# Order of VectorE's low parts and a landing wait on SyncE in the expert stage of a hybrid encoder layer

## The reference

```
expert group = top 1 of 4, then top 2 of its 8 experts, per token
rows sorted by expert, each expert's rows padded to blocks of 128
for each block:  hid = silu(xb @ w_eg[e]) * (xb @ w_eu[e]);   ys = hid @ w_ed[e]
out[token] += ys * gate
```

## Time and profile before

| | |
|---|---|
| time, median of 3 runs | 1236.81 us (1235.13 to 1236.97) |
| the profiled execution | 1234.7 us, span 1232.8 us |
| busy | PE 90%, PEld 78%, DVE 59%, ACT 46%, POOL 26% |
| chain that ended last | PE 78%, DVE 10%, ACT 5% |
| expert stage | from about 804 us to 1189 us of the span |

### The profile page before, as it was taken

One profiled execution on the slowest core, in us unless ns is written; L12 is line 12 of the kernel. 1 busy time (PEld: TensorE's weight loads), 2 busy tenths in 40 slices (PEclk: granted clock), 3 DMA queues, 4 the chain that ended last, 5 costly groups with the idle time before them and its releaser, 6 DMA issues.

```text
span 1232.8 us, 18548 instructions
## 1 busy us (share of the span) xinstructions
PE 1110.1 (90%) x6851; PEld 961.3 (78%) x6851; DVE 730.7 (59%) x948; ACT 563.7 (46%) x759; POOL 325.0 (26%) x273
## 2 busy tenths in 40 slices
PE   3998999999999899999998999758999999999930
PEld 3886888888877788888887788657999999999930
DVE  5874666666044621111113465568888888888838
ACT  5334655665135200000003232336888888888823
POOL 3203222212332223223330000032444444444210
PEclk7998999999999999999999999968999999999975
DMA  8010000020204111111103342348999999999747
GB/s 247 1 28 11 7 7 7 6 70 18 69 1 106 37 29 44 52 52 52 52 12 108 108 171 86 154 175 316 377 373 349 347 347 361 360 379 365 263 153 282
DMA packets 94174, 184.31 MB, mean 150 GB/s; under 512 B 30752, under 2 KB 68128, under 8 KB 80288
## 3 DMA queue, kind: packets, MB, share of 16 engines
q1 hardware_dynamic: 83744, 166.65, 38.9%
q0 software_dynamic: 10368, 16.80, 3.7%
HBM read 177.12 MB, written 27.26 MB: 166 GB/s over the span
## 4 chain that ended last, share of the span: by engine, by line
PE 78%; DVE 10%; ACT 5%; issue 3%; DMA 3%; SPq 1%; POOL 0%; ACTq 0%; DVEq 0%; POOLq 0%
PE ps L376 24%; PE ps L378 23%; PE ps L377 23%; PE ps L900 3%; PE ps L668 2%; DVE pt_lo L1382 1%; PE ps L829 1%; DVE negm L1337 1%; DVE q_tmp L1328 1%; ACT prob L1032 1%; DMA xin<-in_x_dram 1%; DVE acc L1688 1%; DVE res L1698 1%; DVE acc L1689 1%; PE ps L677 1%
## 5 line engine op out<-in xcount | busy, mean ns | idle before, releaser
L1639 DVE TENSOR_TENSOR we_lo<-raw_e,we_hi 128x2048 fp32r<-128x2048 f32 x108 | 246.8, 2287 | 51.2 <-ACT we_hi L1159 51.1
L1159 ACT ACTIVATE we_hi<-raw_e 128x2048 fp32r<-128x2048 f32 x108 | 205.8, 1908 | 0.0
L376 PE MATMUL ps<-ht_hi,w_hi 128*128 128x512 f32 x448 | 176.0, 393 | 0.5 <-DVE ht_lo L1255 0.4
L378 PE MATMUL ps<-ht_hi,w_lo 128*128 128x512 f32 x448 | 174.5, 390 | 0.0
L377 PE MATMUL ps<-ht_lo,w_hi 128*128 128x512 f32 x448 | 174.4, 389 | 0.0
L376 PE MATMUL ps<-we_hi,xst_hi 128*128 128x256 f32 x576 | 169.8, 295 | 1.9 <-DVE xst_lo L1643 1.9
L377 PE MATMUL ps<-we_lo,xst_hi 128*128 128x256 f32 x576 | 163.8, 284 | 0.0
L378 PE MATMUL ps<-we_hi,xst_lo 128*128 128x256 f32 x576 | 163.8, 284 | 0.0
L370 POOL CAST w_hi<-raw 128x1024 fp32r<-128x1024 f32 x36 | 40.5, 1125 | 301.6 <-PE ps L378 268.8
L376 PEld LDWEIGHTS ps<-we_hi,xst_hi 128*128 128x128 f32 x576 | 111.6, 194 | 2.5 <-DVE xst_lo L1643 2.4
L377 PEld LDWEIGHTS ps<-we_lo,xst_hi 128*128 128x128 f32 x576 | 111.4, 193 | 0.0
(11 more groups left out here) (293 smaller groups left out, 2495.8 us busy)
## 6 DMA issues: line engine op xcount, KB each, us to landing
raw_e<-in_w_exp_gate_dram SPq DMA_DIRECT2D x36, 1024.0 KB
raw_e<-in_w_exp_up_dram SPq DMA_DIRECT2D x36, 1024.0 KB
raw_e<-in_w_exp_down_dram SPq DMA_DIRECT2D x36, 1024.0 KB
raw<-in_w_in_dram SPq DMA_DIRECT2D x27, 512.0 KB, 3.8
yin<-y_dram SPq DMA_DIRECT2D x16, 512.0 KB, 6.7
xin<-in_x_dram SPq DMA_DIRECT2D x8, 512.0 KB, 7.0
raw<-in_w_out_dram SPq DMA_DIRECT2D x8, 512.0 KB, 3.9
xre<-in_x_dram SPq DMA_DIRECT2D x8, 512.0 KB, 5.7
```

Source lines behind the costliest of these rows:

```text
L376: pe.matmul(dst, st[0], mv[0], start=first, stop=False)
L378: return pe.matmul(dst, st[1], mv[0], start=False, stop=last)
L1159: act.activation(we_hi[c % 4][:, :], raw_e[c % 6][:, :], ACT.Copy).then_inc(sem("w_hi_ready"), 1)
L1639: dve.tensor_tensor(we_lo[c % 4][:, :], raw_e[c % 6][:, :], we_hi[c % 4][:, :].bitcast(F32), ALU.subtract).then_inc(sem("w_lo_ready"), 1)
```

## The change

On VectorE the low part of the gathered rows (`rows_low`) is no longer the last step of a block for block j + 3: it is now called with j + 2 right behind `hidden_low(it, j)`, ahead of the split of the up piece. Since one block's last step and the next one's first steps follow each other, this is a swap of `rows_low` and `hidden_low`. In the prologue `hidden_low(0, 0)` moves ahead of the split `low(0, 0, 2)`, of `rows_low(0, 2)` and of the gate operations.

On SP, `load` now also waits until piece p - 2 has landed in full before it issues piece p (from the seventh piece on).

```
@@ load, on SP
-                    wait(sp, "w_lo_ready", n - 5)
+                    if isinstance(it, int):
+                        split, arrived = n - 5, (it * 2 + ((c - 2) // 6 + 1)) * 16
+                    else:
+                        split, arrived = sp.to_reg(n - 5), sp.to_reg((it * 2 + ((c - 2) // 6 + 1)) * 16)
+                    if not (isinstance(it, int) and n < 6):
+                        sp.wait_ge(sem(f"raw_e_full{(c - 2) % 6}"), arrived)
+                    wait(sp, "w_lo_ready", split)
@@ expert, on VectorE
-                    hidden_low(it, j)
+                    if not (isinstance(it, int) and it == 0 and j == 0):
+                        hidden_low(it, j)
                     if left(2):
+                        rows_low(it, j + 2)
                         low(1, it, j + 2)
                     if left(1):
                         hidden(it, j + 1)
                         low(2, it, j + 1, not left(2))
                     if left(3):
                         low(0, it, j + 3)
-                        rows_low(it, j + 3)
@@ prologue, on VectorE
                 hidden(0, 0)
                 low(2, 0, 0)
+                hidden_low(0, 0)
                 low(0, 0, 2)
-                rows_low(0, 2)
                 gates()
                 experts(dve, expert)
```

## The result

The changed kernel takes 1258.12 us (median of 4 runs, 1252.86 to 1262.09) beside 1235.97 us of the kernel before (4 runs, 1234.3 to 1236.97): ratio 1.0193, interval 1.015 to 1.0235. It is slower by 22 us, where 9 us faster was forecast, and the range of 1222 to 1240 us doesn't hold it. The profiled execution took 1262.09 us.

What follows compares the result with a forecast made beforehand. TensorE was taken to set the pace, transfers close behind. 4.6 us kept in the loop plus 4.6 at the start, 9.2, off 1234.7 gives 1225.5; the median 2.1 above, 1227.6 us; range 1222 to 1240.

Steps and rivals of the forecast that it cites:

- SP's wait: Issue of weight pieces on SP: waiting for p - 2 costs 0 us on the mean engine.
- 0.8 of one piece was open: SP at 977.0 us, before an issue: issued minus moved bytes, taken to mean p - 2 is home.
- SP's wait empties engines: Rival, loop transfers: share falls to 0.92, 10.5 us an expert, 5 us slower, 1242 us; chance 0.22.
- 7 us of slack: Loop pieces: about 7 of 10.5 us between landing and use, credited against the wait's 17 us loss.
- The order in the loop: VectorE in loop: `hidden_low` ahead of `rows_low` ends the hold at `down`; experts 9.65 to 9.8 us, full value 9.0 us.
- The order at the start: Prologue: earlier `hidt_lo` turns PE's idle 3.80 us into about 1.5 ahead of `rows_in`; gain taken as 4.6 us.
- The transfers take part of it back: Expert loop: transfers let about half the mean DMA idle time be kept, some 4.6 of 9.0 us.
- 10.5 us of slack: Loop pieces: 15.1 us from issue to ScalarE's copy, less 4.6 us landing time.
- the transfers take it back: Rival, loop: last engine already full at 9.95 us per expert; gain 0 to 4.6, about 1234.5 us; chance 0.15.
- nothing else binds: Rival, loop: all 9.0 us come, 13.6 with the start, 1223.2 us; chance 0.15.
- The rows_low is late: Rival: the new order on VectorE makes `rows_low` too late for `rows_in`, near 1237 us; chance 0.03.

Runs made afterwards that it cites:

- order_only: The changed kernel without SP's wait for landed pieces, so only VectorE's new order; 1223.82 us, ratio 0.9923.
- prologue_order: The kernel before with only `hidden_low(0, 0)` moved up in the prologue, loop as before, no wait on SP; 1232.85 us, ratio 0.9998.
- spread_order: order_only with each expert's valid rows spread over the partitions (rank r to slot 8 (r mod 16) + r/16); 1219.04 us, ratio 0.9872.
- wait_p3: The changed kernel with SP waiting for piece p - 3 in place of p - 2; 1226.91 us, ratio 0.992.
- gather_only_wait: The changed kernel, wait on p - 2 kept, with whole gathers but scatters of row 0 only and the combination reading the input; 1220.23 us, ratio 0.9902.
- wait_p4: The changed kernel with SP waiting for piece p - 4 in place of p - 2; 1226.79 us, ratio 0.9938.
- loop_order: The kernel before with only the loop's swap of `rows_low` and `hidden_low`, no wait on SP; 1226.91 us, ratio 0.9933.

## Why the prediction was wrong

**The failed step** is "SP's wait": "A piece alone needs ... say 4.6 us; two in flight allow one per 2.4 us ... Hence 0 us on the mean engine." The form of the sum was right, and its one term was not. The landing time was taken from a piece with no other weight piece under way: SP's issues around it are at 808.61, 818.98 and 828.60. In the loop, beside the row traffic and with two pieces in flight, a landing takes 7.35 us; that is one piece per 3.72 us in place of 2.4, and PE asks for 3.2. The step "0.8 of one piece was open" measured bytes in the mean, and that does not say that p - 2 is home: in order_only 1.5 pieces were open while one issued 15 us earlier had not landed, and in the kernel after 0.3 of a piece just before SP was released. That the rate of two pieces decides is shown from both sides: with few rows a landing takes 4.8 us and nothing is lost; with p - 3 in place of p - 2 each landing takes longer, three are in flight, and nothing is lost.

The rule that spoke against it, of the Trainium skill, "DMA: Bandwidth & Descriptors", section "Why a DMA increments its semaphore by 16 and not by 1", is that the full count comes with the slowest engine. The runs agree that the full landing is what SP pays for: at 1053.8 us most of the bytes are there and SP still waits. They don't tell which engine comes last, nor split the 7.35 us between it and what is common to all; a wait for fewer counts, which might, was not tried.

**The rival "SP's wait empties engines"** is what happened, for its own reason: share 0.90 (it had 0.92), ACT waiting for landings, experts over 10.3 us. Its size was off. It took 10.5 us an expert and 1242 us in all, where the cadence of issues is 11.16 and the result 1258. The 7 us of slack that it credits are about right: (11.16 - 9.62) x 28.3 experts of the chain (85/3) = 44 us. The stage is 36.0 us over order_only's (373.6 - 337.6) and 39.0 over that of spread_order, whose experts take 9.62 throughout, so some 5 to 8 us were covered. That is luck in part: its 10.5 us of slack rest on the same landing of 4.6 us, and no row shows how much of the 15.1 us was landing time in the kernel before. What was off is the term per expert, which took a share of 0.92 for the mean engine and no landing time at all; the share came near it, at 0.90, and the expert did not.

**The order in the loop** was right in mechanism and nearly in size: 9.65 to 9.8 us forecast, 9.62 measured while PE binds, and 0.35 us for the step into `down`, against 0.36.

**The order at the start** was right: 1.59 us idle ahead of `rows_in`, for 1.5, and the clock stayed at 1.00. In order_only this `rows_in` starts at 836.46, 24.56 us after the stage's first; before it was 842.72 - 812.5 = 30.22. That is 5.7 us earlier, for 4.8. What I did not see is that it needs the swap in the loop to be kept (prologue_order).

**The transfers take part of it back** was right in kind, and near in size by luck. 9.2 us was the sum of order alone; order_only's median is 10.7 us under before's of the same time, its stage 11.2. Of the loop's gain the sum kept 4.6 of 9.0, by taking half of the mean idle time, for which no row stood. With the start's 5.7 taken off, order_only keeps 5.5 us of stage in the loop, of the 8.5 that spread_order shows at the same bytes. So what was taken back hung on where the rows lie, and not on the volume. The rival "the transfers take it back" entirely is refuted, and so is "nothing else binds" (13.6), though spread_order reaches it: 14.2 us of stage, 15.0 of median.

**"The rows_low is late"** did not occur beyond the 1.6 us at the start.

With the measured numbers in the prediction's own sum: -11 for the order, and for the wait 44 less the 7 us of slack, makes 26 us slower. Measured were 24.8 of stage and 22 of median. This is hindsight: the 3.72 us a piece is read from the kernel after, and no row of the kernel before holds it.

## What to carry to other kernels

A wait for the landing of piece p - k allows k pieces in flight. It costs nothing as long as k pieces in flight, beside the traffic of the stage and counted to their last part, come as fast as the consumer asks. A landing time from a quiet moment is too short for this (4.6 us for 7.35), and one from a kernel with more in flight is too long (15 to 16 us in order_only, which over two would give some 8 us a piece, where 3.72 was measured): the landing time goes with the window, so k has to be tried, here with k = 2 and k = 3. That SP waits long is no sign of a cost (138 us in wait_p3, 145 in gather_only_wait); the cost shows in the consumers, when copies wait for landings (69.6 us after, 13.6 in wait_p3). And when a stall is removed, follow the engine's queue one iteration further: with the old order behind it, the same stall came back 10 us later.

## What the runs showed of the hardware

- A 1 MB load lands 4.8 to 4.9 us after its issue beside other weights only, and in 7.35 us (mean of 43) beside gathers and scatters that add 12.85 MB to 84.71 in 300 us, at a mean DMA share of 0.90. 15% more bytes go with a landing half as long again; the second also has two pieces in flight all the time. How this divides among engines stays open.
- Landings grow with the pieces in flight: 7.35 us with two, 8.7 to 11.1 with three (wait_p3), 13.2 to 13.8 with four (wait_p4, from 988 us on), 15.0 to 16.1 for gate pieces without the wait (order_only, from 1015 us on). From three on the stage is as long as without the wait, within 1.3 us.
- A piece can be nearly there long before its full count: 0.3 of a piece was open in two at 1053.8 us of the kernel after, and 1.5 in five at 1050.0 of order_only.
- Where the valid rows of a skipping gather and scatter sit among the partitions matters: the first places cost 13.0 us of copies' waits in 70 us, spread ones none, at the same bytes.
- After PE's idle 1.6 us (order_only) the granted clock stayed at 1.00, 2.4 GHz; after 2.5 us (prologue_order) it showed 0.65 in the next 4.2 us, after 2.7 us (loop_order) 0.50, 1.2 GHz, in 836.5 to 842.4 us, after 3.8 us 0.55 in the next 6.3.
